# The last expert block's rows enter the output sums by a matmul from SBUF, in place of a scatter to DRAM; one number per slot in the lists in place of three

## The reference, cut to what matters

```
experts = g_idx * EXPERTS_PER_GROUP + e_loc          # two of 32 for each token
yr      = (silu(xb @ w_gate[e]) * (xb @ w_up[e])) @ w_down[e]
contrib = yr[dest] * w_s[:, None]
y       = segment_sum(contrib, tok_s)                # two terms for each token
out     = x + gt2 * y
```

## Time and profile before

| | us |
|---|---|
| median of three runs | 1114.88 |
| the profiled execution, its own time | 1117.91 |
| its span, first to last instruction | 1115.4 |
| PE busy | 894.3 |
| DVE busy | 318.2 |
| ACT busy | 317.9 |
| POOL busy | 114.5 |
| bytes moved by DMA | 408.52 MB, mean 366 GB/s |

### The profile page before, as it was taken

The page is one execution under the profiler, slowest core; times in us unless marked ns, Lnnn a source line. Parts: engine busy times, 40 slices in busy tenths (PEclk is TensorE's granted clock), DMA queues, the critical chain, the costliest instruction groups (busy, mean ns, idle before and its releaser), DMA issues.

```text
span 1115.4 us, 19228 instructions
## 1 busy us (share of the span) xinstructions
PE 894.3 (80%) x7028; PEld 457.2 (41%) x7028; DVE 318.2 (29%) x717; ACT 317.9 (29%) x983; POOL 114.5 (10%) x173
## 2 busy tenths in 40 slices
PE   5779999998877888889856998777787777777773
PEld 2324535353434435353534554344344434344332
DVE  0342232272655483526371100000000000000005
ACT  3212525262545456343631111110111011110102
POOL 0000112000000000000312121111111111111110
PEclk9889999999988999989987999999999999999995
DMA  9999999999699886799872999999999999999947
GB/s 370 417 404 381 372 390 400 403 391 319 212 394 394 313 301 220 264 383 334 320 303 97 426 425 426 426 427 427 427 425 429 425 425 426 427 428 426 425 194 254
DMA packets 107906, 408.52 MB, mean 366 GB/s; under 512 B 16553, under 2 KB 21290, under 8 KB 92610
## 3 DMA queue, kind: packets, MB, share of 16 engines
q1 hardware_dynamic: 98706, 386.43, 87.8%
q10 hardware_dynamic: 3712, 11.82, 2.7%
q0 software_dynamic: 5424, 9.46, 2.3%
HBM read 400.03 MB, written 15.74 MB: 373 GB/s over the span
## 4 chain that ended last, share of the span: by engine, by line
PE 46%; DMA 37%; DVE 9%; ACT 4%; issue 2%; ACTq 1%; SPq 0%; DVEq 0%; POOLq 0%; POOL 0%
DMA ring<-in_w_up 32%; PE bank L1502 8%; PE bank L1338 8%; PE bank L1255 5%; PE bank L1247 4%; PE bank L1341 3%; PE bank L1275 2%; DMA ring<-in_w_ada 2%; PE bank L1406 2%; PE bank L1523 2%; PE bank L1397 2%; DMA ring<-in_w_in 2%; DVE vP L827 1%; ACT big L613 1%; PE bank L1180 1%
## 5 line engine op out<-in xcount | busy, mean ns | idle before, releaser
L1502 PE MATMUL bank<-ring,big 128*64 128x256 f32 x2048 | 236.4, 385 | 72.7 <-DMA ring<-in_w_up 41.9
L1502 PEld LDWEIGHTS bank<-ring,big 128*64 128x64 f32 x2048 | 149.4, 138 | 172.0 <-DMA ring<-in_w_up 53.7
L1523 PE MATMUL bank<-ring,big 128*64 128x512 f32 x512 | 116.9, 598 | 15.2 <-ACT big L776 15.2
L774 ACT ACTIVATE big<-bank 128x256 f32<-128x256 f32 x32 | 12.3, 384 | 388.1 <-PE bank L1502 388.1
L1124 DVE TENSOR_TENSOR big<-big,bank 128x256 f32<-128x256 f32 x32 | 13.5, 421 | 304.2 <-ACT big L774 304.2
L595 ACT ACTIVATE big<-bank 128x256 f32<-128x256 f32 x128 | 47.8, 379 | 148.9 <-DVE big L859 141.8
L1247 PE MATMUL bank<-ring,part 128*32 128x512 f32 x512 | 71.2, 642 | 9.9 <-ACT big L595 9.8
L1255 PE MATMUL bank<-ring,big 128*16 128x128 f32 x2048 | 72.5, 285 | 0.3
L859 DVE TENSOR_TENSOR big<-bank,cst 128x512 f32<-128x512 f32 x64 | 44.0, 687 | 97.7 <-PE bank L1247 97.3
L613 ACT ACTIVATE big<-big,ebias 128x256 f32<-128x256 f32 x128 | 63.4, 499 | 15.9 <-DVE ebias L884 15.9
L1523 PEld LDWEIGHTS bank<-ring,big 128*64 128x64 f32 x512 | 34.2, 136 | 77.3 <-issue 54.5
(11 more groups left out here) (290 smaller groups left out, 981.9 us busy)
## 6 DMA issues: line engine op xcount, KB each, us to landing
ring<-in_kT SPq DMA_DIRECT2D x256, 256.0 KB, 7.0
ring<-in_v SPq DMA_DIRECT2D x256, 256.0 KB, 8.1
ring<-in_w_gate SPq DMA_DIRECT2D x32, 2048.0 KB, 27.3
ring<-in_w_up SPq DMA_DIRECT2D x32, 2048.0 KB, 27.4
ring<-in_w_down SPq DMA_DIRECT2D x32, 2048.0 KB, 27.2
ring<-in_w_ada SPq DMA_DIRECT2D x12, 2048.0 KB, 13.9
ring<-in_w_in SPq DMA_DIRECT2D x4, 2048.0 KB, 25.8
wbuf<-in_w_in SPq DMA_DIRECT2D x3, 2048.0 KB, 11.9
```

The costliest lines, as they stand in the source:

```text
L1502: last = pe.matmul(B[1 + w][64 * f:64 * f + 64, 0:256], xv[:, c, h, :], wv[:, k, 256 * f:256 * f + 256], start=k == 0, stop=k == KT - 1)
L1523: last = pe.matmul(B[4 + p][64 * h:64 * h + 64, :], av[:, c, f, :], wv[:, k, 512 * h:512 * h + 512], start=k == 0, stop=k == FF // 128 - 1)
```

## The change

**Tail.** The last block (parity 1 of the last pair) is not scattered. `y2` is filled with zeros beforehand by one DMA of 4.7 MB, and SP waits only for the scatters of the blocks before the last one. The last block's rows stay in `Yo[1]` and are added in PE's accumulation: a matrix `spread_last` (128 x 576) holds, for each of its rows, the gate weight in the column of its token. To make that possible the turn of `yc` becomes a matmul with the identity, and eight matmuls over 64 rows follow it. The last pair is taken out of the loop on POOL, DVE and PE.

```diff
-            for p in range(2):
-                sp.wait_ge(y_scat[p], 16 * n_pair + 16)
-            for p in range(2):
-                sp.sem_inc(s["settle"], 1)
-                sp.wait_ge(gathered[p], 16 * n_pair + 16 * (2 - p))
+            sp.wait_ge(y_scat[0], 16 * n_pair + 16)
+            sp.wait_ge(y_scat[1], 16 * n_pair)
+            sp.sem_inc(s["settle"], 1)
             for t in range(TT):
...
+            for p in range(2):
+                sp.sem_inc(s["settle"], 1)
+                sp.wait_ge(gathered[p], 16 * n_pair + 16 * (2 - p))
```

SP, after the loads of the second expert and before the loop of loads:

```diff
+            sp.wait_ge(s["zeroed"], 5)
+            sp.dma_start(y2.rearrange("(p j) n -> p j n", p=128), zeros.unsqueeze(1).to_broadcast([128, 4 * NT // 128, 512]))\
+                .then_inc(s["filled"], 16)
```

PE, for each group t of tokens:

```diff
+                if t == 0:
+                    pe.wait_ge(s["last_spread"], 3)
+                    pe.wait_ge(s["y_out"], 2 * n_last + 4)
-                for k in range(KT):
-                    last = pe.transpose(B[2 * (t % 2) + k // 4][:, 128 * (k % 4):128 * (k % 4) + r],
-                                        yc[t % 2][0:r, 128 * k:128 * k + 128], C["ident"][0:r, 0:r])
-                    if k % 4 == 3:
-                        last.then_inc(s["c_turned"], 1)
+                for c in range(4):
+                    for h in range(2):
+                        to = B[2 * (t % 2) + h][:, 128 * c:128 * c + r]
+                        col = 512 * h + 128 * c
+                        pe.matmul(to, yc[t % 2][:, col:col + 128], C["ident"][:, 0:r], start=True, stop=False)
+                    for h in range(2):
+                        last = pe.matmul(B[2 * (t % 2) + h][:, 128 * c:128 * c + r],
+                                         Yo[1][64 * h:64 * h + 64, 128 * c:128 * c + 128],
+                                         spread_last[64 * h:64 * h + 64, 128 * t:128 * t + r], start=False, stop=True)
+                        if c == 3:
+                            last.then_inc(s["c_turned"], 1)
```

```diff
-            then(dve.tensor_tensor(rows, C["iota"].unsqueeze(1).unsqueeze(1).to_broadcast([128, 2 * TT, 2, RB]),
+            then(dve.tensor_tensor(rows, C["iota"].unsqueeze(1).to_broadcast([128, 2 * TT, RB]),
...
-            for c in range(2):
-                ins = dve.tensor_tensor(blks[:, :, 1 + c, :], blks[:, :, 0, :],
-                                        pay[:, :, c:c + 1].to_broadcast([128, 2 * TT, MAXBLK]), ALU.mult)
-                ins.then_inc(s["listed"], 1)
+            dve.tensor_tensor(blks[:, :, 1, :], blks[:, :, 0, :],
+                              C["payload"].unsqueeze(2).to_broadcast([128, 2 * TT, MAXBLK]), ALU.mult).then_inc(s["listed"], 1)
...
+            then(dve.tensor_scalar(nint[0:1, 3 + NOV:4 + NOV], npf[0:1, 1:2], float(NE // 2 - 1), None, ALU.add))
...
+            dve.wait_ge(s["lists_summed"], 1)
+            dve.tensor_scalar(back, named, 2.0 * NT + 1, -2.0 * NT, ALU.is_gt, ALU.mult)
+            then(dve.tensor_scalar(free, named, 1.0, C["dump"], ALU.is_lt, ALU.mult))
+            then(dve.scalar_tensor_tensor(scat, named, C["half"], free, ALU.add, ALU.add))
+            then(dve.tensor_tensor(tblS[:, 0, 0:MAXBLK], scat, back, ALU.add))
+            then(dve.tensor_copy(tblS[:, 1, 0:MAXBLK], scat))
+            dve.sem_inc(s["listed_rows"], 1)
...
+            dve.tensor_tensor(blks[:, :, 2, :] ..., blks[:, :, 0, :] ..., wts ..., ALU.mult).then_inc(s["weights_listed"], 1)
+            dve.wait_ge(s["weights_summed"], 1)
+            then(dve.tensor_copy(wtab, B[3][:, 0:MAXBLK]))
```

PE, for the lists:

```diff
-            for x in range(2 * TT):
-                last = pe.matmul(B[5][:, 0:3 * MAXBLK], rows[:, x, :, :].rearrange("p h r -> p (h r)"),
-                                 blks[:, x, :, :].rearrange("p c b -> p (c b)"), start=x == 0, stop=x == 2 * TT - 1)
+            def list_sum(bank, c):
+                for x in range(2 * TT):
+                    for h in range(2):
+                        last = pe.matmul(bank[64 * h:64 * h + 64, 0:MAXBLK], rows[:, x, :], blks[:, x, c, :],
+                                         start=x == 0, stop=x == 2 * TT - 1)
+                return last
+            pe.wait_ge(s["listed"], 1)
+            list_sum(B[5], 1).then_inc(s["lists_summed"], 1)
+            pe.wait_ge(s["count_ready"], 1)
+            pe.wait_ge(s["weights_listed"], 1)
+            list_sum(B[3], 2).then_inc(s["weights_summed"], 1)
```

More of the change, by code:

```diff
@@ L236, in build_kernel @@
         six = [topi[:, 2 + i:3 + i] for i in range(2)]
+        spread_last = big[:, 5120:5120 + NT]
+        count2 = big[:, 5120 + NT:5120 + 2 * NT]
+        wtab = big[:, 5120 + 2 * NT:5120 + 2 * NT + MAXBLK]
+        last_two = topf[:, 0:2]
+        zeros = uxr[:, 0:512]
         yb = [[ring[:, (2 * i + j) * 1024:(2 * i + j + 1) * 1024] for j in range(2)] for i in range(TT)]
@@ L454, in _, with pool_expert @@
                 pool.dma_start(first[:, 2 * p:2 * p + 2], d["consts"][p:p + 1, 0:2]).then_inc(y_scat[p], 16)
-            with pool.Fori(0, n_pair) as i:
-                for p in range(2):
[L458 to L473, removed]
+            def pool_expert(i, p, last):
+                q = 1 - p
+                pool.wait_ge(gathered[q], 16 * i + 16 * (p + 1))
+                stage(gix[q][:, :], tblS[:, 0, ds(2 * i + (p + 3), 1)], 4 * i + (2 * p + 4))
+                pool.wait_ge(s["x_turned"], 2 * i + p + 2)
+                pool.sem_inc(s["settle"], 1)
+                gather(q)
+                if last:
+                    return
+                pool.wait_ge(y_scat[p], 16 * i + 16)
+                stage(six[p][:, :], tblS[:, 1, ds(2 * i + p, 1)], 4 * i + (2 * p + 5))
+                pool.wait_ge(s["y_out"], 2 * i + p + 3)
+                pool.wait_ge(y_scat[1 - p], 16 * i + 16 * (p + 1))
+                pool.sem_inc(s["settle"], 1)
+                pool.indirect_dma_start(y2, bass.IndirectOffsetOnAxis(six[p][:, :], 0), Yo[p], None,
+                                        bounds_check=4 * NT - 1, oob_is_err=False)\
+                    .then_inc(y_scat[p], 16)
@@ L1130, in combine @@
+            with dve.Fori(0, n_last) as i:
+                for p in range(2):
+                    dve_expert(i, p)
+            dve.wait_ge(s["last_spread"], 2)
+            dve.wait_ge(s["placed"], 14)
+            dve.tensor_scalar(spread_last, count2, last_two[:, 0:1], last_two[:, 1:2], ALU.is_equal, ALU.mult)\
+                .then_inc(s["last_spread"], 1)
+            for p in range(2):
+                dve_expert(n_last, p)
             def combine(t):
@@ new lines, in pe_expert @@
+            def pe_expert(i, p):
+                xv = XT[p].rearrange("q (c h r) -> q c h r", c=4, h=2)
+                pe.wait_ge(s["xT_ready"], 2 * i + p + 1)
+                for w in range(2):
+                    pe.wait_ge(e_full[p][w], 16 * i + 16)
+                    wv = eslot[p][w].rearrange("q (k n) -> q k n", k=KT)
+                    for k in range(KT):
+                        h, c = divmod(k, 4)
+                        for f in range(2):
+                            last = pe.matmul(B[1 + w][64 * f:64 * f + 64, 0:256], xv[:, c, h, :],
+                                             wv[:, k, 256 * f:256 * f + 256], start=k == 0, stop=k == KT - 1)
+                    if w == 0:
+                        last.then_inc(s["gate_done"], 1)
+                last.then_inc(s["gate_up"], 1)
+                pe.wait_ge(gathered[1 - p], 16 * i + 16 * (p + 1))
+                turn_rows(1 - p)
+                pe.wait_ge(s["act_ready"], 2 * i + p + 1)
+                for c in range(2):
+                    last = pe.transpose(B[3][:, 128 * c:128 * c + 128], aa[p][:, 128 * c:128 * c + 128], C["ident"])
+                last.then_inc(s["a_turned"], 1)
+                pe.wait_ge(s["aT_ready"], 2 * i + p + 1)
+                pe.wait_ge(e_full[p][2], 16 * i + 16)
+                pe.wait_ge(s["y_out"], 2 * i + p + 1)
+                av = aT[p].rearrange("q (c f r) -> q c f r", c=2, f=2)
+                wv = eslot[p][2].rearrange("q (k n) -> q k n", k=FF // 128)
+                for k in range(FF // 128):
+                    f, c = divmod(k, 2)
+                    for h in range(2):
+                        last = pe.matmul(B[4 + p][64 * h:64 * h + 64, :], av[:, c, f, :], wv[:, k, 512 * h:512 * h + 512],
+                                         start=k == 0, stop=k == FF // 128 - 1)
+                last.then_inc(s["down"], 1)
@@ L1526, in _ @@
+            with pe.Fori(0, n_last) as i:
+                for p in range(2):
+                    pe_expert(i, p)
+            for p in range(2):
+                pe_expert(n_last, p)
             for t in range(TT):
```

136 lines of the change are left out of this document (57 added, 79 removed).

## The result

The changed kernel takes 1124.23 us (median of 7 runs, 1122.40 to 1126.58), the kernel before in the same series 1114.79 (7 runs, 1112.11 to 1119.52): the ratio is 1.0082, with a 95% interval of 1.0065 to 1.0099. It is slower by 9.4 us (difference of the medians), where 1105.0 was forecast, in a range of 1101.5 to 1112.0. The profiled execution has a span of 1123.7 us and a time of 1125.57.

What follows compares the result with a forecast made beforehand. Stream start, set by the lists, and the tail's wait and DVE were taken to bound the kernel. Lists 3.2 plus tail 6.7 (8.9 - 0.7 - 1.5) give 9.9 us less: 1105.0 us, range 1101.5 to 1112.

Steps and rivals of the forecast that it cites:

- steps 1 to 6: Making of the lists, ahead of the weight stream: smaller one-hot rows, shorter sums, covered second sum; POOL's first copy 3.4 us earlier.
- The fill: Zeroing `y2` by DMA in the empty stretch before the first gather: 11.1 us long, 0.2 us taken off for it.
- rival D: Fill of `y2` outlasts the empty stretch and delays the third expert's weights: slower, 1126 at 100 GB/s; chance 0.05.
- Step 8: Tail: SP waits for the scatter before the last, so `y2` loads and DVE's first sums come 8.9 us earlier.
- step 10: Tail: PE at half clock needs 5.4 us per group; one such stretch costs about 1.5 us, between 0 and 3.
- step 9: Tail: PE's 16 matmuls per group take 2.9 us at full clock, covered except in the last group, 0.7 us more.
- Rival A: PE sets the tail's pace at half clock, 5.4 us per group, the last about 4.7: 1113.9; chance 0.12.
- rival A's price of 4.6 us: PE's group at full clock if transposes are four times as fast: time about 1110; 0.02 of A's chance.
- step 6: Lists: PE's new second sum, of the weights, is covered by 1.1 us; with a 4.5 us first sum it costs 0.9.
- the low bound of the seam: Least gain of lists and fill together, 1.2 us (slow sum, no cover, late fill), where 3.2 was forecast.

Runs made afterwards that it cites:

- the kernel with the lists alone: Changed kernel with the old tail (last block scattered and waited for, eight transposes per group, no fill of `y2`): 1111.54 us, ratio 0.9969 to the kernel before.
- grouped order: Changed kernel with the same 16 matmuls per group, the identity's eight first, then the eight over 64 rows: 1105.64 us, ratio 0.9900 to the kernel before.
- held clock: Changed kernel with three 128x512 matmuls into an unread bank, in PE's gap before the first group: 1108.83 us, one run.
- Grouped transposes: Changed kernel with eight transposes per group first, then the eight 64-row matmuls adding to them: 1104.02 us, ratio 0.9899 to the kernel before.
- transposes alone: Changed kernel with eight transposes per group for the 16 matmuls, last block's rows left out of the sums: 1101.19 us, ratio 0.9884 to the kernel before.

## Why the prediction was wrong

**Right.** The lists (steps 1 to 6): the stream starts 2.7 us earlier, 3.2 forecast, and the kernel with the lists alone is 3.5 faster than before in its own series. The fill (nearly covered by the empty stretch, 0.6 to 1.0 us for the 0.2 forecast; rival D did not come). Step 8, the early start: 9.5 us at PE's first group, 8.9 forecast, and no load of `y2` stood in the way of a weight. With PE's part made cheap the forecast sum holds: 1101.2 without the last block's rows, 1104.0 and 1102.6 with them. The grouped order is the kernel that the prediction had in mind: 3.15 us of PE per group and one stretch at half clock, and it takes 1105.6, where 1105.0 was forecast.

**Wrong: step 10, the clock.** The forecast took one stretch at half clock and 1.5 us, because "a PE that needs 5.4 us for what DVE gives it every 3.3 is busy throughout" and such stretches had brought the clock up in the earlier trace rows. PE was busy throughout, as said, for 36 us, and the clock stayed at half for all but the first 1.2. The row it leaned on shows transposes in an unbroken run of one kind. The held clock is worth 15.4 us of the 19.2 between forecast and result (14.9 by the tails). PE's busy time in these rows does not tell the cases apart: it was busy 3.40 of 3.40 us in the change and in the grouped order, with the clock at half behind the one and full behind the other. It is not chance either, as the mean clocks of the seven executions of the one (0.944 to 0.950) and the four of the other (0.960 to 0.967) lie apart. The order of the matmuls decides it here; what in the order does so stays open, as no run took it apart.

**Wrong: step 9, PE's work per group.** 2.9 us at full clock was 4.25, and 5.4 at half was 7.5. With the clock held, the 4.25 against DVE's 3.3 make most of the other 3.8 us of the miss. The instruction prices themselves were right: 0.107 each at full clock, and 64-row ones in pairs. Missing was what it costs to go between 128-row and 64-row matmuls, eight times per group: about 0.2 us each at full clock, and at half clock (7.5 - 5.1) / 8 = 0.3. The pair in the earlier trace rows stands in a run of its own and could not show it. That it is the going between the kinds that costs is read from these prices in the three orders; why it costs is not shown. Rival A had the clock right and carried only the error of this step: with four groups of 7.5 us and a last of 6.7 for its 5.4 and 4.7 it gives 1124.3. That this meets the median so well is in part luck: in the profile the first group, begun at full clock, took 6.6, and the wait gave 9.5 for 8.9, so that the profile lies 8.3 us above the one before and not 9.4.

The rule that the full clock does not come for transposes (the Trainium skill, TensorE: Matmul & The Clock Gate, Part 4: PE-mode transpose) would have made the new tail, all matmuls proper, fast sooner, and it was not: mixed column by column, they did not bring the clock back in 36 us. Grouped transposes with the 64-row matmuls did, at 1081.7; transposes alone, 1.97 us of each 3.3, stayed at half. The factor of two between a transpose and a matmul with the identity, which rival A's price of 4.6 us put in doubt, holds at full clock: eight transposes take 1.02 us to the start of the next kind, and the identity's sixteen instructions 1.98.

Two slips in the sums changed nothing. In step 6 a slow second sum is priced at 0.9 us, but with the first sum as slow the table is late too and it is 1.5, so the low bound of the seam was 0.6 and not 1.2. In step 10, 1.7 us lost less 0.5 of slack is 1.2, not 1.5.

## What to carry to other kernels

Price a string of small matmuls by its order, not by its count: matmuls over all rows and over half of them each in a run of their own, and a term for each change between the two. Where PE sets the pace behind a gap of a few us, ask whether its own work can bring the clock back, and do not take its being busy for an answer. Filling the gap with work nobody reads held the clock here (three matmuls, 14.9 us off the tail). A start moved ahead by 9.5 us is worth that only if the engine behind it has the slack for what made the move possible.

## What was not expected of the hardware

The same instructions have two steady paces: 1.06 us per column tile if they begin at full clock and 1.88 if they begin at half, each for the whole tail (21 and 36 us). Changing their order takes 18.6 us off. And eight useless matmuls in the critical path, 8.7 us long, made the tail 6.2 us shorter, in one profile of each. A matmul can add onto what a transpose has left in PSUM, which no row of the kernel before shows.
